# Turning the unscaled x by matmuls with a scaled diagonal at the start of a two-block transformer kernel

## The reference, cut to what matters

```
def rms_norm(x, gain):
    xf = x.astype(jnp.float32)
    y = xf * lax.rsqrt(jnp.mean(xf * xf, axis=-1, keepdims=True) + EPS)
    return (y * gain.astype(jnp.float32)).astype(x.dtype)

hn = rms_norm(h, attn_norm[layer])            # h = x for layer 0
q, f, i, g = jnp.split(hn @ w_in, 4, axis=-1) # hgrn2_mixer
```

## Time and profile before

| what | value |
|---|---|
| median of 3 executions | 1610.45 us (1610.41 to 1611.73) |
| profiled execution, its own time | 1610.3 us |
| profiled execution, its span | 1608.5 us |
| TensorE busy | 1583.5 us, 98% |
| VectorE busy | 1187.8 us, 74% |
| ScalarE busy | 856.4 us, 53% |

### The profile page before, as it was taken

The page is one execution under the profiler, slowest core; times in us unless marked ns, Lnnn a source line. Parts: engine busy times, 40 slices in busy tenths (PEclk is TensorE's granted clock), DMA queues, the critical chain, the costliest instruction groups (busy, mean ns, idle before and its releaser), DMA issues.

```text
span 1608.5 us, 25574 instructions
## 1 busy us (share of the span) xinstructions
PE 1583.5 (98%) x9761; PEld 1365.1 (85%) x9761; DVE 1187.8 (74%) x1795; ACT 856.4 (53%) x1204; POOL 79.2 (5%) x28
## 2 busy tenths in 40 slices
PE   9999999999999999999999999999999999999998
PEld 7887888889888888888889788888888888788887
DVE  5996787887577888766689776667666676876665
ACT  5444655565465557544465864447444475464443
POOL 0000000003500000000008200000000000000000
PEclk9999999999999999999999999999999999999999
DMA  9624557763336555555657245654656563445552
GB/s 295 214 86 131 186 184 218 209 166 138 119 131 209 183 177 189 196 183 189 229 141 239 79 147 195 194 206 147 209 184 203 198 207 114 156 144 185 194 195 79
DMA packets 215198, 283.39 MB, mean 176 GB/s; under 512 B 13260, under 2 KB 183235, under 8 KB 215123
## 3 DMA queue, kind: packets, MB, share of 16 engines
q1 hardware_dynamic: 213635, 278.18, 53.1%
q10 hardware_dynamic: 1488, 4.17, 0.8%
HBM read 280.88 MB, written 1.44 MB: 176 GB/s over the span
## 4 chain that ended last, share of the span: by engine, by line
PE 91%; DVE 5%; ACT 2%; issue 1%; DMA 0%; DVEq 0%; ACTq 0%
PE ps L2239 25%; PE ps L2246 13%; PE ps L2010 13%; PE ps L2011 13%; PE ps L2012 13%; PE ps L2022 2%; PE ps L2017 2%; PE ps L2018 2%; PE ps L2144 1%; DVE w_lo L1317 1%; DVE x_pair L1224 1%; ACT arena L659 1%; DVE ps L1882 1%; PE ps L2392 1%; PE ps L2551 1%
## 5 line engine op out<-in xcount | busy, mean ns | idle before, releaser
L610 ACT ACTIVATE w_hi<-raw 128x2048 fp32r<-128x2048 f32 x255 | 484.9, 1909 | 169.4 <-PE ps L2246 95.4
L1395 DVE TENSOR_TENSOR w_lo<-raw,w_hi 128x2048 fp32r<-128x2048 f32 x162 | 371.0, 2290 | 188.4 <-ACT w_hi L610 188.4
L2239 PE MATMUL ps<-x_pair,w_hi 128*128 128x512 f32 x1792 | 427.1, 390 | 0.0
L2239 PEld LDWEIGHTS ps<-x_pair,w_hi 128*128 128x128 f32 x1792 | 332.6, 188 | 66.6
L2246 PEld LDWEIGHTS ps<-x_pair,w_lo 128*128 128x128 f32 x1792 | 229.8, 191 | 8.8
L2246 PE MATMUL ps<-x_pair,w_lo 128*128 128x256 f32 x1792 | 232.4, 283 | 0.0
L1317 DVE TENSOR_TENSOR w_lo<-raw,w_hi 128x2048 fp32r<-128x2048 f32 x80 | 182.4, 2287 | 43.8 <-ACT w_hi L610 42.7
L2010 PE MATMUL ps<-w_hi,g_hi 128*128 128x512 f32 x480 | 187.5, 391 | 0.0
L2011 PE MATMUL ps<-w_lo,g_hi 128*128 128x512 f32 x480 | 187.5, 391 | 0.0
L2012 PE MATMUL ps<-w_hi,g_lo 128*128 128x512 f32 x480 | 186.7, 389 | 0.0
L2010 PE MATMUL ps<-x_pair,w_hi 128*128 128x256 f32 (+1 forms) x552 | 157.1, 285 | 0.4 <-issue 0.3
(11 more groups left out here) (202 smaller groups left out, 1888.4 us busy)
## 6 DMA issues: line engine op xcount, KB each, us to landing
raw<-in_ffn_w_in SPq DMA_DIRECT2D x80, 1024.0 KB, 5.1
raw<-in_ffn_w_out SPq DMA_DIRECT2D x44, 1024.0 KB, 4.9
raw<-in_ffn_w_up SPq DMA_DIRECT2D x40, 1024.0 KB, 5.1
raw<-in_ffn_w_down SPq DMA_DIRECT2D x22, 1024.0 KB, 5.0
raw<-in_hgrn_w_in SPq DMA_DIRECT2D x16, 1024.0 KB, 8.0
raw<-in_gla_w_in SPq DMA_DIRECT2D x12, 1024.0 KB, 5.5
raw<-in_ffn_w_in SPq DMA_DIRECT2D x16, 512.0 KB, 4.5
raw<-in_dsa_w_in SPq DMA_DIRECT2D x6, 1024.0 KB, 6.1
```

The costliest lines, as they stand in the source:

```text
L610: act.activation(w_hi[slot][:, :], raw[slot][:, :], ACT.Copy).then_inc(hi_done[slot], 1)
L1395: dve.tensor_tensor(w_lo[slot][:, :], raw[slot][:, :], w_hi[slot][:, :].bitcast(F32), ALU.subtract)\
L2239: pe.matmul(ps[:, bank, :], w_hi[s][:, at:at + P], x_pair[:, k, :, :].rearrange("p x t -> p (x t)"), start=k == 0, stop=False, skip_group_ ...
```

## The change

`first_scale` is a new area of 2 x 128 words. The two blocks of x are no longer scaled in `xn`. VectorE writes instead, for each block, a 128x128 diagonal with the inverse norms of the block's tokens, and TensorE multiplies each 128x128 chunk of x itself with it: the product is the turned and scaled chunk. In block 1, ScalarE squares and sums the second half alone; the mean square of the first half is made by VectorE from `bn_stats` and `bn_aggr` (mean and variance) as variance plus the square of the mean. These stand ahead of `add_eps(0)` in VectorE's list. One product of zeros less stands ahead of the turning.

```
+        first_scale = words(2048, NTB * P)
...  ScalarE
-            for tb in range(NTB):
-                square_first(tb)
+            square_first(0)
+            act.wait_ge(x_in[1], 16)
+            act.sem_inc(rms_sq, 1)
+            square_half(1, 1, h[:, 1, 512:1024], D ** -0.5)
+            root_of_sum(1)
...  VectorE
+            dve.wait_ge(x_in[1], 16)
+            link(dve.bn_stats(ln_stats[:, 0:6], h[:, 1, 0:512]))
+            link(dve.bn_aggr(ln_mv[:, 0:2], ln_stats[:, 0:6]))
+            link(dve.scalar_tensor_tensor(ln_mv[:, 2:3], ln_mv[:, 0:1], ln_mv[:, 0:1], ln_mv[:, 1:2], ALU.mult, ALU.add))
+            add_eps(0, EPS)
+            want(rms_sq, 2)
+            dve.tensor_scalar(ssq_eps[:, 1:2], ln_mv[:, 2:3], 0.5, EPS, ALU.mult, ALU.add).then_inc(rms_eps, 1)
             dve.wait_ge(first_in, 2 * 16)
             for tb in range(NTB):
-                scaled_block(tb)
+                r = inverse_rms(tb)
+                dve.tensor_scalar(first_scale[:, tb * P:tb * P + P], ident, r, None, ALU.mult).then_inc(xn_ready, 2)
...  TensorE
+            def turn_scaled(tb):
+
+                pe.wait_ge(xn_ready, want(xn_ready, 2))
+                for c in range(NK):
+                    at = tb * SEQ + c % 2 * P
+                    ins = pe.matmul(ps[:, 4 + c // 2, at:at + P], h[:, tb, c * P:c * P + P], first_scale[:, tb * P:tb * P + P],
+                                    start=True, stop=True, skip_group_check=True)
+                    if c % 2 == 1:
+                        ins.then_inc(turned, 1)
...
-            keep_warm(6)
-            turn_block(0)
-            turn_block(1)
+            keep_warm(5)
+            turn_scaled(0)
+            turn_scaled(1)
```

## The result

The changed kernel took 1612.83 us in the median of 20 executions (1612.35 to 1614.38), the kernel before 1611.68 us in 20 executions beside it (1610.12 to 1612.26). The ratio of the means is 1.0013, with a 95% interval of 1.0007 to 1.0019: about 2.1 us slower. The profiled execution took 1612.85 us and has a span of 1611.1.

A forecast was written before the change was run, and what follows sets the result against it. TensorE, busy 98% of the span, was taken to bound the kernel, so a later first three-part product delays everything: +1.51 us on the 1610.45 median gives 1612.0. The range was 1610.4 to 1613.5.

The forecast's parts named there:

- both strands: VectorE's path to w_lo[1] and TensorE's slab 0 matmuls, forecast to let the first three-part product start at 18.93.
- +1.51 us: Forecast delay of the first three-part product, from 17.42 to 18.93, passed on whole to the span; chance 0.82.
- within 0.2%: Result within 3.2 us, taken as about what a measurement can tell from no change; chance 0.92 less 0.01.
- 0.6 to 2.2: Forecast's own range in us for the start's shift, from other turning pitches, bn_stats times and diagonal times: 1611.1 to 1612.7.
- 8.31: Forecast time when TensorE starts turning block 0: its root at 7.43 plus 0.88 for reciprocal, diagonal and links.
- 11.88: Forecast end of turning block 1, after block 0 from 8.31 to 10.09, when the slab 0 matmuls begin.
- the shift of the start: Later start of TensorE's first three-part product; span growth by anything else was to prove the prediction wrong.
- The clock: Rival: TensorE's clock falls in the new gap, 6.81 to 8.31; turning takes 3.57 us more, 1615.5; chance 0.06.
- the gap at 131.54: Evidence against a clock fall: after 1.95 us of TensorE idleness, 512-column matmuls followed at full pitch, 0.23.
- Four transposes' price for a float32 product: Rival in the turning: 16 products at 0.544 each add 5.1 us to the 1.51, giving 1617.1; chance 0.02.
- Statistics in time: Rival: x's second block lands at 4.80, root 0 stays at 6.12; 0.9 us faster, 1609.5; chance 0.03.
- A swallowed shift: Rival: a later TensorE wait, set by a transfer or another engine, absorbs the delay; 1610.45; chance 0.07.

The follow-up runs named there:

- eps_first: The changed kernel with one line moved: block 0's add of EPS ahead of the wait for x's second block; lower group of times 1611.8 us.
- turn_cheap: The changed kernel with transposes of unscaled x in place of products with the diagonal, leaving the scaling out; lower group of times 1611.4 us.
- stats_only: Against the kernel before, only the statistics part of the change, with the old scaling and turning; lower group 1611.7 us, ratio 1.0005.
- before_filled: The kernel before with 15 instead of 7 products of zeros ahead of the first output projection; lower group 1610.4 us, ratio 0.9996.
- diag_only: The changed kernel without the statistics: ScalarE squares both halves of both blocks, turning by products with the diagonal; lower group 1610.75 us, ratio 1.0002.
- diag_filled: The diagonal alone, without the statistics, with 15 instead of 7 products of zeros ahead of the first output projection; lower group 1610.75 us.
- stats_eps_first: The statistics part alone with block 0's add ahead of the wait for the load, old scaling and transposes; lower group 1611.0 us.
- after_start_idle: The changed kernel with 15 products of zeros ahead of the first output projection and none ahead of the turning; ten executions, 1614.27 to 1616.76 us.

## Why the prediction was right or wrong, point by point

**The place and the direction were right.** Block 0's add queued behind the wait for the load, ScalarE stuck at that root, block 1's root later in spite of the saved square, the turning unbroken and ordered by TensorE, both strands arriving together: each is in the profile. eps_first shows the first link by itself, turn_cheap the last.

**Two steps failed.** The first is the one that turned a sum of +1.51 us into a forecast of no change: "A change of 0.2%, 3.2 us, is about what a measurement of this kernel can tell from none." Twenty executions of each kernel gave an interval of 0.06%, about 1 us, to either side. By it the measured 2.1 us is clearly slower, and my own 1.51 would have been too. I put about 0.92 on "within 0.2%"; the ratio is within 0.2%, and it still is a change.

The second is the size of the sum, 1.51 us forecast against 2.16 in the trace and 2.2 by groups. The 0.6 to 2.2 that I wrote down for it holds 2.16, but that is luck, since its ends don't follow from its terms. The lowest ones together give 0.64 - 0.20 - 0.14 = 0.30, and the highest ones 1.64 + 0.19 = 1.83 (a pitch of 0.236 gives 1.64, not 1.7), and 2.16 lies above. What was mis-sized is the way up to TensorE's first product, 8.31 forecast and 8.86 measured, the pitch behind it, and a pause that stood nowhere in the sum:

- The load landed at 6.39, not 6.10. In the other thirteen profiles in which VectorE waits for it, it was there between 6.07 and 6.35, 6.17 in the middle, so that about 0.1 of this 0.29 is usual and the rest chance.
- `scalar_tensor_tensor` on one column took 0.22, not 0.15 to 0.17, and from the end of the add to the root it was 0.10, not 0.04. With links and the rest of the statistics that is 0.13.
- From a root's start to TensorE it was 1.01, not 0.88: 0.40 to the reciprocal (0.33 forecast) and 0.27 from there to the diagonal (0.20 forecast).
- Behind it, 0.229 a chunk instead of 0.223 adds 0.10. 0.29 + 0.13 + 0.13 + 0.10 is the 0.65 between 11.88 and 12.53.
- 0.3 to 0.4 us at 127.7, VectorE's pause ahead of L1639, was not forecast at all. I had said that the prediction is wrong if the span grows by something other than the shift of the start; in this part it does. The pause is in the profiles of stats_only, turn_cheap and all filled versions of the changed kernel, and not in those of before, before_filled, diag_only and diag_filled. In eps_first and stats_eps_first there is no idle time at this place either, but the eight instructions of L1639 take 2.31 instead of 2.16. eps_first has the same VectorE instructions as the changed kernel, with one of them moved. What the pause waits for is open.

**The clock was the rival that I priced too low.** It had 0.06. Of 26 executions of the changed kernel filled at 130, nine lay above 1614 (8 of 22, and one of the four single ones), and the one that was caught shows the clock down behind the new gap. It is no part of the 2.2 us, which is the distance between the lower groups. My evidence against it, the gap at 131.54 that left the clock alone, was one execution of something that turns out to go either way: about half of the executions of the kernel before lie 1.6 us higher, and filling that gap ends it. Its price, 3.57 us, was too large, since the clock came back before the turning was over (granted clock 0.83 from 11.8 to 12.8 and 1.00 behind it): 1.5 to 1.7 us. The unfilled changed kernel has both gaps, and I can't say which of its upper executions fell at which.

**The other rivals.** Four transposes' price for a float32 product is excluded by the 0.229 a chunk. Statistics in time: the load landed too late, and stats_eps_first shows that even with the add out of the way VectorE makes it a loss of 0.43. A swallowed shift: no.

**What the two parts cost.** The diagonal alone is 0.29 (0.41 between the filled kernels, 17.86 against 17.45), the statistics alone 1.00, together 2.16 (1.9 to 2.0 with the load of the other profiles). They are more than a sum, because a late block 0 is hidden with transposes (1.09 for a block) and not with products (1.83 for a block, ahead of all of block 1).

None of the versions of the changed beginning beat the kernel before. The one that may be better is the kernel before with the gap at 130 filled: it keeps the 1610.4 of the lower group in all of eleven executions, though its ratio of 0.9996 (0.9987 to 1.0005) doesn't tell it from the kernel before.

## What to carry to other kernels

Work that is put ahead of a small instruction in an engine's list delays everyone who waits for that instruction: here a wait for a load and 1.2 us of statistics, meant to save ScalarE 0.6, held up a 0.15 us add, and through it a root, a square and a second root. A dearer product is free only while TensorE has idle time in front of the critical block; look whether the next block must queue behind it. And sort the times before comparing medians: in the kernel before, two groups 1.6 us apart came from the clock behind a TensorE gap of 1.95 us, and eight more products of zeros removed them. And before a forecast calls a change too small to be measured, work out from the times at hand how wide the interval will be.

## What the runs showed of the hardware that I had not expected

- A TensorE gap of 1.95 us in front of the first output projection is followed by a granted clock of 0.50 for 3.4 us in some executions (profiles of stats_only and stats_eps_first) and by the full clock in others: 48 of 98 executions of the kernel before lay in the group 1.6 us higher, and none of eleven with the gap filled. The fall came 0.5 us after TensorE had gone back to work in one profile and 1.4 us after in the other.
- The same was caught once behind a gap of 1.86 us at 7 us into the program, while gaps of 1.86 and 1.89 at the same place left the clock alone.
- In the first microseconds the granted clock reads 1.00 in every profile, although the first products of zeros run at 0.42 us each, the lower level, and in after_start_idle it does so while 32 records take 6.03 us instead of 3.84. Where the clock matters, the pitch of like instructions is the surer reading.
- The second 512 KB load of x landed between 6.07 and 6.39 us with the same instructions ahead of it, which in the changed kernel, where the chain of the start hangs on this load, shifts the whole program by as much.
